# All mixer weight chunks as three rounded passes, split in half chunks over three slots, remainders by GpSimd

## What is computed

```
for l in range(DEPTH):                       # DEPTH = 2
    h = rmsnorm(x, norm_mix_g[l])
    z = h @ w_in[l]                          # 1024 x 8968
    z_a, z_b, z_c, z_dz, z_dxbc, z_ddt, z_g = split_cols(z, IN_SPLITS)
    y_a = mixer_spatial_gating(z_a, ...)     # A
    y_b = mixer_pool(z_b, ...)               # B
    y_c = mixer_rwkv7(z_c, ...)              # C, a scan over time, done in 2 blocks of 128
    y_d = mixer_ssd(z_dz, z_dxbc, z_ddt, ...)  # D
    proj = einsum('btkc,kcd->btkd', stack([y_a, y_b, y_c, y_d]), w_branch[l])
    merged = sum_k sigmoid(z_g)_k * proj_k
    x = x + merged @ w_out[l]
    h = rmsnorm(x, norm_ffn_g[l])
    x = x + (swiglu(h, ...) if l == 0 else moe_swiglu(h, ...))
return rmsnorm(x, norm_final_g)
```

## Time and profile before

| | us |
|---|---|
| median of 3 runs | 2362.6 (2359.48 to 2362.95) |
| the profiled execution, span | 2358.8 |
| PE matmul busy | 2247.5 (95%) |
| DVE busy | 1481.9 (63%) |
| ACT busy | 1031.5 (44%) |
| POOL busy | 51.6 (2%), 52 instructions |
| layer 0: token mixer, first projection matmul to the end of the output projection | 21.5 to 509.5 |
| layer 0: dense channel mixer | 520.5 to 766 |
| layer 1: token mixer | 780.5 to 1270.6 |
| layer 1: norm, router and experts | 1276 to 2334 |

### The profile page before, as it was taken

How to read it: one execution, slowest core, us unless ns; L and a number is a source line. 1 busy time by engine, 2 the same in 40 slices (tenths; PEclk the granted TensorE clock), 3 DMA queues, 4 the chain that set the end, 5 groups by cost and what they waited for, 6 DMA issues and landing times.

```text
span 2358.8 us, 31394 instructions
## 1 busy us (share of the span) xinstructions
PE 2247.5 (95%) x12248; PEld 1840.1 (78%) x12248; DVE 1481.9 (63%) x1571; ACT 1031.5 (44%) x846; POOL 51.6 (2%) x52
## 2 busy tenths in 40 slices
PE   7979999989999897999997899999999999999997
PEld 6968889879999786888986677777777777777775
DVE  3544655236553453565422688888888888888885
ACT  4322100123332432210011476777777767777773
POOL 0100000000000010000000000000000000000000
PEclk9989999989999998999998799999999999999998
DMA  7423212325454342311132398989999989989892
GB/s 295 176 72 118 79 54 72 127 105 189 172 190 179 125 143 72 127 70 61 66 108 90 145 369 330 367 339 356 351 346 350 348 347 351 366 330 366 330 368 113
DMA packets 69345, 504.69 MB, mean 214 GB/s; under 512 B 7696, under 2 KB 7952, under 8 KB 8208
## 3 DMA queue, kind: packets, MB, share of 16 engines
q1 hardware_dynamic: 68832, 500.57, 56.7%
q10 hardware_dynamic: 432, 2.95, 0.3%
HBM read 502.44 MB, written 1.05 MB: 213 GB/s over the span
## 4 chain that ended last, share of the span: by engine, by line
PE 93%; DVE 4%; ACT 1%; issue 1%; DMA 0%; SPq 0%; DVEq 0%; ACTq 0%
PE g L433 61%; PE m L433 31%; PE m L899 1%; DVE h L1343 1%; DMA ring<-stream 0%; DVE arena L1561 0%; DVE rstd L1341 0%; PE m L466 0%; DVE arena L1559 0%; ACT w_high L1156 0%; ACT L1005 0%; DVE rstd L1438 0%; ACT arena L1002 0%; DVE h L1868 0%; DVE small L1451 0%
## 5 line engine op out<-in xcount | busy, mean ns | idle before, releaser
L1747 DVE TENSOR_TENSOR ring_low<-ring,we_high 128x2048 fp32r<-128x2048 f32 x336 | 769.0, 2289 | 153.7 <-ACT we_high L1201 153.1
L1201 ACT ACTIVATE we_high<-ring 128x2048 fp32r<-128x2048 f32 x336 | 644.2, 1918 | 273.9 <-PE g L433 181.0
L433 PE MATMUL g<-we_high,hg_high 128*96 128x512 f32 x896 | 358.6, 400 | 10.3 <-DVE ring_low L1747 10.3
L433 PE MATMUL g<-ring_low,hg_high 128*96 128x512 f32 x896 | 353.9, 395 | 0.0
L433 PE MATMUL g<-we_high,hg_low 128*96 128x512 f32 x896 | 352.7, 394 | 0.0
L433 PE MATMUL g<-h,ring 128*128 128x256 f32 x1472 | 337.5, 386 | 0.0
L433 PE MATMUL m<-arena 128*128 128x128 f32 (+7 forms) x2152 | 297.3, 302 | 21.1 <-DVE arena L1417 9.3
L433 PEld LDWEIGHTS g<-h,ring 128*128 128x128 f32 x1472 | 281.8, 194 | 42.0 <-issue 4.3
L433 PEld LDWEIGHTS m<-arena 128*128 128x128 f32 (+3 forms) x2152 | 269.7, 192 | 48.9 <-issue 14.8
L433 PE MATMUL g<-h_high,w_high 128*128 128x256 f32 x768 | 220.1, 287 | 26.1 <-DVE h_low L1664 24.1
L433 PE MATMUL g<-h_high,ring_low 128*128 128x256 f32 x768 | 219.6, 286 | 0.0
(11 more groups left out here) (240 smaller groups left out, 2340.7 us busy)
## 6 DMA issues: line engine op xcount, KB each, us to landing
ring<-stream SPq DMA_DIRECT2D x472, 1024.0 KB, 4.8
cc<-cc_in SPq DMA_DIRECT2D x1, 2352.5 KB, 16.3
sw<-sw_in SPq DMA_DIRECT2D x1, 1088.0 KB, 11.1
sw<-sw_in ACTq DMA_DIRECT2D x1, 1088.0 KB, 6.8
x<-x_in SPq DMA_DIRECT2D x1, 1024.0 KB, 4.9
out<-h ACTq DMA_DIRECT2D x1, 1024.0 KB, 3.9
rep<-rep_in SPq DMA_DIRECT2D x1, 768.0 KB, 17.7
rep<-rep_in ACTq DMA_DIRECT2D x1, 768.0 KB, 8.2
```

The source lines that it names most:

```text
L433: return pe.matmul(o, a, b, start=start, stop=stop, skip_group_check=True)
L1201: A(we_high[n % 3][:, :], ring[:, slot, :], ACT.Copy).then_inc(high_ready, 1)
L1747: TT(ring_low[:, slot, :], ring[:, slot, :], we_high[n % 3][:, :], ALU.subtract).then_inc(low_ready, 1)
```

## The change

Only the two token mixers change in substance; the dense mixer and the experts keep their code (with `w_high` at another address and `high_ready` counted from zero).

- All 47 chunks of a mixer layer go through `three`. The unit of splitting is a half chunk (HALF = 1024 columns); the rounded halves lie in `z_w`, three slots of 1024, in place of `w_high`'s two of 2048. A slot comes free when PE has used the half three before (`half_free`; `half_used` counts first halves, `chunks_used` whole chunks).
- ACT makes all high halves, 94 a layer in place of 12 whole chunks (`z_high(l, n, b)`), in the order of the stream, at fixed places of its program (`z_highs(l, upto)`): around each evacuation, and inside `gates`, where the loop at quarter q4 first makes the halves below 2 NZ + q4 // 2 + 3, so two beyond the one that PE works on.
- The low halves of the first 12 chunks stay with DVE. The 70 of the other 35 chunks go to POOL (`lows`), with B's pooling, the additions into `mg` for steps 2 to 5 (`adds`) and the low parts of the branch outputs A, B and D (`y_lows`) at fixed places among them.
- The branch outputs are split too: ACT writes `y_high` (`y_split`), the low part overwrites the output. For C, DVE does it at once behind `yC`. The merged sum gets `mg_high` from ACT and `mg_low` from DVE; the additions of steps 6 and 7 move from POOL to DVE. The output projection runs its halves in the order (0,0), (1,0), (0,1), (1,1), then in order, so that the first two need only half of `mg`.
- The 8-column dt projection is split as well, and moves from behind chunk 1 to behind chunk 4.
- To make room: constants `count`, `reset`, `sel` are made on the chip (two memsets on POOL, one copy on DVE), arena regions move, `h_low` overwrites `h`; the rep DMA of layer 1 is issued later.

```
+        def half_free(eng, l, n, b):
+            at = 2 * (l * N_MIX + n) + b - N_SLOTS
+            if at >= 0:
+                before, m, half = at // (2 * N_MIX), at % (2 * N_MIX) // 2, at % 2
+                if half:
+                    eng.wait_ge(chunks_used, chunk0(before) + m + 1)
+                else:
+                    eng.wait_ge(half_used, before * N_MIX + m + 1)
...
             def evacuate(l, units):
                 for unit in units:
                     name, i = unit
+                    n = Z_UNITS.index(unit)
+                    z_highs(l, 2 * n + 4)
                     act.wait_ge(chunks_used, unit_chunk(l, unit) + 1)
...
                     q.add(ins, g_drained[G_PLAN[unit][0]])
+                    z_highs(l, 2 * n + 5)
...
             def gates(l, lo, hi):
+                for q4 in range(lo, hi):
+                    (step, i), part = MERGE_CHUNKS[q4 // 4], q4 % 4
+                    z_highs(l, 2 * NZ + q4 // 2 + N_SLOTS)
+                    if (step, i) == (6, 2) and part == 0:
+                        y_split(l, 2)
...
+                    if (step, i) == (2, 0):
...
+                        y_split(l, 1)
+                    if (step, i) == (4, 0):
...
+                        y_split(l, 3)
...
+                gates(l, SIDE_END, 12 * STEPS)
+                z_highs(l, 2 * (NZ + N_MERGE) + 3)
+                for i in range(4):
+                    act.wait_ge(merged, 2 * STEPS * l + 13 + i)
+                    A(mg_high[:, 2 * i:2 * i + 2, :], mg[i], ACT.Copy).then_inc(S["mg_high_ready"], 1)
+                z_highs(l, 2 * N_MIX)
...
+            def lows(l, lo, hi):            # POOL
+                for n in range(lo, hi):
+                    for b in range(2):
...
+                        pool.wait_ge(z_high_ready, 2 * (l * N_MIX + n) + b + 1)
+                        G.tensor_tensor(half_ring(ring_low, l, n, b), half_ring(ring, l, n, b), half_slot(l, n, b), ALU.subtract)\
+                            .then_inc(pool_low_ready, 1)
...
             def merge(l):                    # PE
                 merge_quarters(l, SIDE_END, 12 * STEPS)
-                for i in range(N_OUT):
-                    w = chunk(chunk0(l) + NZ + N_MERGE + i)
-                    if i == 0:
-                        pe.wait_ge(merged, 2 * STEPS * (l + 1))
-                    g_free(pe, l, ("out", i))
+                for i, b in ((0, 0), (1, 0), (0, 1), (1, 1), (2, 0), (2, 1), (3, 0), (3, 1)):
+                    wh, wl = halves(l, NZ + N_MERGE + i, b)
...
+                            if i == 0 and j == 0 and k % 2 == 0:
+                                pe.wait_ge(S["mg_low_ready"], 4 * l + kt // 2 + 1)
```

More of the change, by code:

```diff
@@ L93 @@
 CC_LIST = [("ones", T), ("eps", 1), ("gn_eps", 1), ("ident", P), ("heads", P), ("strict_up", P), ("incl_up", P), ("low2", P), ("up2", P),
-           ("off", LEVELS * P), ("count", 4 * T), ("reset", 4 * T), ("sel", H * P), ("slots", CAP), ("slot", 1)]
+           ("off", LEVELS * P), ("slots", CAP), ("slot", 1), ("count", 4 * T), ("reset", 4 * T), ("sel", H * P)]
+WINDOWS = (2, 4, 8, 16)
+EARLY = 16
 CC, _n = {}, 0
@@ L717, in merge_quarters @@
                     (step, unit), part = MERGE_CHUNKS[n // 4], n % 4
-                    w = chunk(chunk0(l) + NZ + n // 4)
+                    half, quarter = part // 2, part % 2
+                    wh, wl = halves(l, NZ + n // 4, half)
                     if unit < 2:
@@ L722, in merge_quarters @@
                             g_free(pe, l, ("gate", step, unit))
-                        j = part // 2
-                        for k in range(4 * (part % 2), 4 * (part % 2) + 4):
-                            last = mm(gb(("gate", step, unit))[:, j * T:(j + 1) * T], w[:, DT * j + k, :], h[:, k, :],
-                                      k == 0, k == DT - 1)
+                        for k in range(4 * quarter, 4 * quarter + 4):
+                            last = three(gb(("gate", step, unit))[:, half * T:(half + 1) * T], wh[:, quarter, k % 4, :], wl[:, quarter, k % 4, :],
+                                         h_high[:, k, :], h_low[:, k, :], k == 0, k == DT - 1)
                     else:
@@ L740, in merge_quarters @@
-                        if part % 2 == 0:
-                            g_free(pe, l, ("pj", step, part // 2))
+                            if branch == 2:
+                                pe.wait_ge(S["yc_low_ready"], 2 * (l + 1))
+                            else:
+                                pe.wait_ge(S["y_low_ready"], 2 * (3 * l + step // 2 + 1))
+                        if quarter == 0:
+                            g_free(pe, l, ("pj", step, half))
                         for k in range(4):
-                            last = mm(gb(("pj", step, part // 2))[:, (part % 2) * T:(part % 2 + 1) * T], w[:, 4 * part + k, :],
-                                      ys[branch][:, k, :], k == 0, k == 3)
@@ L745, in merge_quarters @@
-                    if part == 3:
-                        last.then_inc(chunks_used, 1)
+                            last = three(gb(("pj", step, half))[:, quarter * T:(quarter + 1) * T], wh[:, quarter, k, :], wl[:, quarter, k, :],
+                                         y_high[:, k, :], y_low[branch][:, k, :], k == 0, k == 3)
+                    if quarter:
+                        half_over(last, half)
             def merge(l):
                 merge_quarters(l, SIDE_END, 12 * STEPS)
-                for i in range(N_OUT):
-                    w = chunk(chunk0(l) + NZ + N_MERGE + i)
-                    if i == 0:
-                        pe.wait_ge(merged, 2 * STEPS * (l + 1))
-                    g_free(pe, l, ("out", i))
-                    for j in range(2):
-                        for k in range(DT):
-                            last = mm(gb(("out", i))[:, j * T:(j + 1) * T], w[:, DT * j + k, :], mg[:, k, :],
-                                      k == 0, k == DT - 1)
-                    last.then_inc(chunks_used, 1)
+                for i, b in ((0, 0), (1, 0), (0, 1), (1, 1), (2, 0), (2, 1), (3, 0), (3, 1)):
+                    wh, wl = halves(l, NZ + N_MERGE + i, b)
+                    if b == 0:
+                        g_free(pe, l, ("out", i))
+                    for j in range(2):
+                        for k in range(4):
+                            kt = 4 * b + k
+                            if i == 0 and j == 0 and k % 2 == 0:
+                                pe.wait_ge(S["mg_low_ready"], 4 * l + kt // 2 + 1)
+                            last = three(gb(("out", i))[:, j * T:(j + 1) * T], wh[:, j, k, :], wl[:, j, k, :],
+                                         mg_high[:, kt, :], mg_low[kt // 2][:, kt % 2, :], kt == 0 and j == 0, kt == DT - 1)
+                    half_over(last, b)
@@ L1158, in split_h, with y_split @@
+            highs = [0]
+            def y_split(l, branch):
+                for i in range(2):
+                    if branch == 2:
+                        act.wait_ge(S["yc_ready"], 2 * l + i + 1)
+                    two = slice(2 * i, 2 * i + 2)
+                    A(y_high[:, two, :], (yA, yB, yC, yD)[branch][:, two, :], ACT.Copy).then_inc(S["y_high_ready"], 1)
             def split_h(n):
```

283 lines of the change are left out of this document (184 added, 99 removed).

## The result

| | before | after |
|---|---|---|
| median of 4 runs, us | 2361.7 (2359.5 to 2363.0) | 2384.8 (2383.4 to 2386.3) |
| span of the profiled execution, us | 2358.8 | 2384.5 |
| mean granted clock | 0.962 | 0.947 |

The change makes the kernel slower by 1.0%: ratio 1.0102, 95% interval 1.0088 to 1.0117. The forecast was 2356 us, so its direction was wrong. The time stands beside that of the second rival, the one by the port (2387). The third rival has the same time, but its condition, halves of POOL over 2.8 us, does not hold (2.47 on the average).

The account below looks back on a forecast made before the run. PE was taken as the bound, 93% of the chain that ended last. Gains 26.9 less losses 23.5 gave 3.4 us a layer, 7 in all: span 2352, median 2356 us, likeliest 2343 to 2370, range 2325 to 2390.

Parts of the forecast that it names:

- second rival: Both mixers: the port costs each DVE operation a whole POOL operation; some 15 us a layer more, 2387 us; chance 0.15.
- third rival: Rounding makes POOL's low half longer than 2.8 us; at 3.1 each, 31 us in all, 2387 us; chance 0.12.
- Gains: Per layer: levels 10.2, nine chunks 10.4, c chunk in D 1.0, start 1.4, output projection 3.9; sum 26.9 us.
- branch A: DVE's chain from the norm to `vn_ready`, meeting POOL: loss of 0 to 4 us a layer, taken as 1.2.
- Can POOL follow?: POOL's low half 2.43 us against PE's 2.88, so POOL hides; first half behind its pooling 0 to 1, taken as 0.
- ACT's order: bo and kt: High halves stand behind ACT's waits for `ss_ready` and `ab_ready`; PE idles in bo and before kt: loss 9.8 us a layer.
- I take about a half.: Where DVE and POOL meet: between a free pass and a whole 2.35 us for each DVE operation, about half.
- The token shift: DVE's 3.89 + 5.63 us beside POOL: best case PE gains 4.6, worst it stalls 8; taken 0 net.
- yC: Yc's tail, three DVE operations while POOL makes the last halves: loss of 0 to 7 us a layer, taken 3.0.
- the masks: C's masks ahead of each block, 10 DVE operations: loss of 0 to 7 us a layer, taken 2.4.
- The clock: Lower granted clock behind PE's waits: 2.7 us at kt, 2.3 at yC, 2.3 at the output projection.
- The rule weighed: DVE instructions with two SBUF inputs and GpSimd ones reading SBUF exclude each other for the whole instruction; sum 2386 us.

Follow-up runs that it names:

- experiment 2: Kernel before the change, eight unused 128x1024 POOL subtractions added beside DVE's token shift: 2373.5 us; the same work in 32 pieces of 128x256: 2360.9 us.
- experiments 2 and 3: The second of these: changed kernel with each POOL low half cut into two instructions of 512 columns, 2382.2 us, or four of 256, 2374.2 us.

## Why the prediction was wrong, step by step

- **Gains.** Right. The levels' quarters gave 9.3 of 10.2, chunk `ss` 1.2, the output projection with the last two 3.4 of 3.9, the start with dt 1.5 of 1.4. One part was no gain: a chunk that ends at a wait for DVE gives nothing, as branch A shows.
- **"Can POOL follow?"** Its low half was 2.35 to 2.47 as taken; the third rival is out. "0 to 1, taken as 0" for the first half behind the pooling held too. But I looked only at what POOL delivers, not at what it meets.
- **ACT's order: bo and kt.** Right in mechanism and nearly in size: 9.8 forecast, 8.3 measured; kt's gap 9.6 where I had said some 9; the gap in bo 2.2, where I had 2.5. The low clock behind the gap cost 1.7, where I had 2.7.
- **ACT's order: the v chunks.** The step is missing. I went through ACT's evacuations from branch D on, and took the first twelve chunks as unchanged because DVE still makes their low halves. But their slots changed too, from two whole chunks to three halves, and ACT's wait for both v chunks kept back the halves behind them: 3.0 us of PE's wait, 3.3 a layer by experiment.
- **The conv.** Missing as well: PE waits 2.5 us for its silu. I said nothing of DVE's conv, since before the change POOL is idle there. The rule that I had weighed would have told that low halves of the first c chunks, and the pooling behind them, meet its last pass.
- **"I take about a half."** This is the step that failed. The token shift was forecast 0 net ("in the best case PE gains 4.6, in the worst it stalls 8"); it cost 8.4. Branch A was 1.2 of 0 to 4; its segment cost 4.3 more than that. yC was 3.0 of 0 to 7; DVE lost 5.5 us (10.7 from the operation behind the reciprocal to yC, in place of 5.2), and the segment cost 2.1 more than forecast. At all of these POOL had its next half queued, so the upper end was the likely one. The three make 14.8 of the 20.8 us by which layer 0 missed its forecast, enough alone to turn the 3.4 gained into a loss; the v chunks and the conv make most of the rest. For the masks, where POOL had no half queued throughout, even the half was more than they cost (1.5 and 0.4 against 2.4).
- **The clock.** I counted 2.7 and 2.3 us of low clock behind the waits at kt and yC (1.7 and 2.0 measured), and none at the token shift, where a wait of 4.8 brought 4.1 more (experiment 2 shows the same on the kernel before).
- **The rule weighed.** The Trainium skill (SBUF — State Buffer, Who interferes with whom) says that the two exclude each other for the whole instruction. The traces agree: 2.5 and 2.6 us for operations of 0.47 beside a half of 2.35, and 3.39 for one of 1.22. By that rule the sum was 2386, and 2384.8 was measured; I had the row for it and took half of it, with 0.15 on that rival. But the sum agrees by luck in part: it holds neither the v chunks nor the conv, and it has 6 a layer at the masks, where 1.5 and 0.4 were measured.
- **Sums that don't come out.** The second rival's terms (2.8, 5, 3.6, 4 and 0.9) make 16.3 a layer and not "some 15": 2389 us. PE's arrival at kt, "+29.2", is 28.2 by its own terms, and 28.4 in the trace. Neither changes the forecast.

## What to carry to other kernels

Before giving an idle GpSimd work, list what VectorE does beside it with SBUF operands, and price each meeting at one whole GpSimd instruction if GpSimd has its next one queued: here the bill was at most the smaller of the two counts times that instruction. Then place the work where VectorE is idle or reads PSUM, hold it back with a wait where VectorE's chain is what others wait for, or let VectorE do it itself: 1.15 us of its own was cheaper than meeting 2.35 of GpSimd. And price a wait of TensorE with the slower matmuls behind it.

## What the runs showed of the hardware that I had not expected

- **Strict turns.** With both queues full, DVE and POOL alternate by instruction (experiments 2 and 3). Pieces of half the size gave nothing clear of noise, since thirteen operations of the token shift met one in place of eight; pieces of a quarter gave 10.6 us.
- **Who takes part.** Operations of DVE with one tensor from PSUM do not meet POOL: the levels' masks keep their 690 ns in the changed kernel, also the twelve of them (over both layers) that ran wholly beside a busy POOL.

```profile
L1686 DVE TENSOR_TENSOR arena<-m,cc 128x512 f32<-128x512 f32 x24 | 16.6, 690 | 14.0 <-PE m L463 13.9
```

  TENSOR_SCALAR, with a single tensor from SBUF, does: 0.40 us alone, 2.3 and 2.5 beside a low half. But the reciprocal, also with one tensor from SBUF, does not: it takes 6.55 us as before, and POOL's first two halves in the second row, 2.42 us each, fall within it:

```profile
464.27 6.55 DVE L1725 RECIPROCAL arena<-arena 128x1024 f32<-128x1024 f32 x1 [7.15 <-ACT arena L1166]
```

```profile
465.19 13.00 POOL L1395 TENSOR_TENSOR ring_low<-ring,z_w 128x1024 fp32r<-128x1024 f32 x5 [1.22 <-ACT z_w L1199]
```

  The same page of the Trainium skill counts `tensor_scalar` among the operations that can take the shared pair. The reciprocal isn't in its list; by its rule a DVE instruction with at most one SBUF input, outside the modes that use two ports, doesn't contend, and the rows agree for this shape.
- **POOL pays too.** Behind DVE's 3.9 us difference one low half took 5.33 us. In turns with DVE's short operations it paid little: a half took 2.5 to 2.6 us in place of 2.35 to 2.4, and a piece of 256 columns 0.68 in place of 0.61 (experiment 2). The kernel before has 0.64 for that size:

```profile
L1312 POOL TENSOR_TENSOR arena<-arena,cc 128x256 f32<-128x256 f32 x4 | 2.5, 636 | 0.3
```

- **Rounded output costs POOL nothing**: 2.35 us for a half written in the rounded format, 2.35 for the plain one.
